# Moving the matmuls of a batch's value compression from the end of the batch before into three places of the batch's own first half

## The chip, the cores and the metric

The kernel runs on one core of one Trainium2 chip. The metric is the device time of one execution in microseconds, as the median of three runs. Everything is float32.

## The reference, cut to what matters

One inference step of a two-layer hybrid decoder, for a prompt of 512 tokens and a sample group of 8 batches with 8 new tokens each, on 2,048 past tokens. In every layer the sample group does, batch by batch, two kinds of attention:

```python
kvc = compress(gather(pool_cmp) + new, pe, w1, w2)     # 127 compressed keys and values from 16 pages
o_cmp, o_sel = nsa_global(q, pos, kvc, blocks)         # compressed scores choose 16 of 32 blocks, selected attention
o_win = window_sample(q_a, win_all)                    # last 512 rows
o_dil = dilated_sample(q_b, dil_all)                   # (128,1), (512,4), (2048,16)
y = merge(o_cmp, o_sel, o_win, gate, o_dil, w_out)

def compress(kv, pe, w1, w2):                          # separately for keys (s=0) and values (s=1)
    hid = silu(sum over 32 positions of (kv + pe) @ w1)
    return hid @ w2
```

The compressed keys are needed for the scores, and the scores for the choice of blocks. The compressed values are needed only for the last product of the compressed branch, `p_cmp @ kvc_values`.

## The kernel before, in words

Each layer has a projection, the prompt's attention (4 rounds of 12 steps), 8 batches of the sample group, and 36 units of output projection and MLP. The five engines run their own programs, written out by hand, and meet on counting semaphores. No scheduler decides an order: what stands first in an engine's program is done first, and a wait holds up all that is behind it on that engine.

For each batch TensorE (the PE rows) does, in this order: dilated scores of the first nine tiles (L1371), scores with the new keys (L1388), compressed keys (L1395) and values (L1401) from the hidden layer, compressed scores (L1408), window scores (L1409), new scores (L1412, L1413), the last four dilated tiles (L1371), the sum for the block choice (L1421), a transpose (L1425), selected scores in two halves (L1431), transposes of the window's probabilities (L1441) and the dilated ones (L1449), dilated outputs (L1463, with L1457 among them), compressed and window outputs (L1470 to L1473), transposes of the selected probabilities (L1480), selected outputs (L1496) and the placing of all outputs (L1508, L1513).

`compress(s, lo, hi, at)` (L1303) is the large product of the compression, `raw pages @ w1`. It is 16 steps of two matmuls for the keys (s = 0) and as many for the values (s = 1). The trace counts two PE records for each of these matmuls, so one compression is 64 records. Both compressions of batch b + 1 stand in the second half and at the end of batch b. Behind each, ScalarE takes an exponential (L744) and VectorE makes the hidden layer with an addition, a reciprocal and a product (L1935, L1937, L1939), which raises `h_done`. Those of the first batch of a layer stand among the last steps of the prompt's attention.

The raw pages of a batch lie in one buffer, `raw`, half of the tile `ring` (2 MB). There is no second one. SyncE (the SP queue) loads it. Its loop per batch is:

```python
page = page_numbers(b + 1)                              # 16 register loads
sp.wait_ge(h_full.sem, h_full.at(it, 2))                # both compressions of batch b have read raw
load_raw(page, range(0, 9))
sp.wait_ge(td_full.sem, td_full.at(it, TD_SD + 1))
load_dilated_k(b + 1)                                   # 1280 KB and 1024 KB
load_raw(page, range(9, NPG))
sp.wait_ge(win_pv.sem, ...); sp.wait_ge(od_full.sem, ...)
load_window(b + 1); load_dilated_v(b + 1, ...)
sp.wait_ge(oa_full.sem, ...); load_selected(page)
```

`h_full` is raised by the last matmul of each compression, once for the keys and once for the values of a batch. TensorE waits for all 16 pages (`raw_ld`) ahead of the first matmul of the next batch's key compression. The last four dilated key tiles are loaded by ScalarE's queue (L758), once the first five are used.

Of the kernel before, what the change touches and what calls it, by code (L numbers as in the profile page):

```python
# [22 lines left out]
ALU = mybir.AluOpType  # L23
ACT = mybir.ActivationFunctionType
# [3 lines left out]
P = 128  # L28
# [4 lines left out]
NB, NS = 8, 8  # L33
# [5 lines left out]
HD = 64  # L39
# [36 lines left out]
STEPS, ROUNDS = STEPS_A + STEPS_D, 4  # L76
# [5 lines left out]
TD_SD, TD_PTC, TD_PTW, TD_PTD, TD_PTS, TD_N = 0, 1, 2, 3, 4, 6  # L82
SC_KTC, SC_VC, SC_S, SC_WIN, SC_NEW, SC_IMP, SC_SEL, SC_LEAST, SC_SUM, SC_OUT, SC_N = (
    0, 1, 2, 3, 4, 5, 6, 8, 9, 10, 11)
SC_BANK = {SC_KTC: 2, SC_VC: 3, SC_S: 4, SC_WIN: 5, SC_NEW: 2, SC_IMP: 3, SC_SEL: 2, SC_SEL + 1: 3,
           SC_LEAST: 2, SC_SUM: 2, SC_OUT: 6}
HID_BANK, FIRST_HID = (4, 5), (2, 3)
EX_CMP, EX_WIN, EX_DIL, EX_SEL = 1, 2, 3, 4
# [96 lines left out]
def build(nc, i, o):  # L185
    ctx = ExitStack()
    with ctx:
# [23 lines left out]
        w2 = sb("w2", P, 2, HD)  # L211
# [350 lines left out]
        def _(act):  # L562
# [168 lines left out]
            with act.Fori(0, DEPTH) as l:  # L731
# [6 lines left out]

                def hidden_exp(it, at):

                    for s in range(2):
                        act.wait_ge(h_full.sem, h_full.at(it, s + 1))
                        act.wait_ge(h_done.sem, h_done.at(it, s))
                        nc.scalar.activation(  # L744
                            he.rearrange("p (k n) -> p k n", k=2),
                            bank[at[s]][:, 0:258].rearrange("p (k n) -> p k n", k=2)[:, :, 1:129],
                            ACT.Exp, scale=-1.0, bias=ncbias[:, s:s + 1]).then_inc(s_hexp.sem, 1)

                def batch(b):
# [14 lines left out]
                    act.wait_ge(td_used.sem, td_used.at(it, TD_SD + 1))  # L764
                    probs(s_d, 3, slice(0, P))
                    act.wait_ge(td_full.sem, td_full.at(it, TD_PTW + 1))
                    B = bank[TD_PTW % 2]
# [11 lines left out]

                hidden_exp(l * NB, FIRST_HID)  # L780
                with act.Fori(0, NB - 1) as b:
                    batch(b)
                    hidden_exp(l * NB + b + 1, HID_BANK)
                batch(NB - 1)
# [202 lines left out]
        def _(pe):  # L987
# [320 lines left out]
            def prompt_steps(l, g, first, last, ends):  # L1308

                for m in range(first, last):  # L1310
                    if m < STEPS or not ends:
                        step_scores(l, *in_round(g, m))
                    if m == 5:
                        chunk_scores(l, g)
                    if m >= TO_T and (m - TO_T < STEPS or not ends):
                        step_transposes(l, *in_round(g, m - TO_T))
                    if ends and m == STEPS:
                        pe.wait_ge(a_sb.sem, a_sb.at(l, 2 * STEPS_L))
                        pe.wait_ge(raw_ld.sem, raw_ld.at(l * NB, NPG))
                        pe.sem_inc(waits_taken_pe, 1)  # L1320
                        compress(0, 0, 4, FIRST_HID[0])
                    if ends and m == STEPS + 1:
                        compress(0, 8, 12, FIRST_HID[0])
                    if ends and m == STEPS + 2:
                        compress(1, 0, 4, FIRST_HID[1])
                    if m == 9:
                        chunk_probs_transposes(l, g)
                    if m >= TO_PV:
                        step_outputs(l, g, m - TO_PV)
                    if ends and m == STEPS:  # L1330
                        compress(0, 4, 8, FIRST_HID[0])
                    if ends and m == STEPS + 1:
                        compress(0, 12, 16, FIRST_HID[0])
                    if ends and m == STEPS + 2:
                        compress(1, 4, 8, FIRST_HID[1])
                    if m == 10:
                        chunk_outputs(l, g)
# [4 lines left out]
            with pe.Fori(0, DEPTH) as l:  # L1342
# [14 lines left out]
                def batch(it, more):  # L1357
# [39 lines left out]
                    last.then_inc(sc_full.sem, 1)  # L1397
                    pe.wait_ge(h_done.sem, h_done.at(it, 2))
                    B = bank[SC_BANK[SC_VC]]
                    for k in range(2):  # L1400
                        last = mm(B[:, k * HD:(k + 1) * HD], hid[:, 1, k * P:(k + 1) * P], w2[:, 1, :],  # L1401
                                  start=(k == 0), stop=(k == 1), skip_group_check=True)
                    last.then_inc(sc_full.sem, 1)

# [8 lines left out]
                    mm(B[low, 64:128], q_a, kns[:], start=True, stop=True, skip_group_check=True).then_inc(  # L1413
                        sc_full.sem, 1)

                    pe.wait_ge(kda_ld.sem, kda_ld.at(it, 2))
# [7 lines left out]
                    pe.sem_inc(waits_taken_pe, 1)  # L1424
                    tr(bank[TD_PTC % 2][:, 0:64], s_c, ident[0:64, 0:64]).then_inc(td_full.sem, 1)  # L1425

                    pe.wait_ge(sel_ld.sem, sel_ld.at(it, NPG))
                    for u in range(2):
                        pe.wait_ge(sc_used.sem, sc_used.at(it, (SC_NEW, SC_IMP)[u] + 1))
                        for h, rows in enumerate((low, high)):  # L1430
                            last = mm(bank[SC_BANK[SC_SEL + u]][rows, :], q_a,  # L1431
                                      kvsel[:, 8 * h + 4 * u:8 * h + 4 * u + 4, 0:128], start=True, stop=True,
                                      skip_group_check=True)
                        last.then_inc(sc_full.sem, 1)
                    pe.wait_ge(s_exp.sem, s_exp.at(it, EX_WIN))
                    pe.wait_ge(td_used.sem, td_used.at(it, 1))
# [36 lines left out]
                    mm(O[high], ptw[0:64, 4, :], vsm[:, 128:256], start=False, stop=True,  # L1473
                        skip_group_check=True).then_inc(win_pv.sem, 1)

# [10 lines left out]
                    if more:  # L1486
                        pe.wait_ge(raw_ld.sem, raw_ld.at(it + 1, NPG))
                        compress(0, 0, 3, HID_BANK[0])
                    O = bank[3][:, 0:P]
# [12 lines left out]
                    if more:  # L1502
                        compress(0, 3, 11, HID_BANK[0])
                    B = bank[SC_BANK[SC_OUT]]
# [44 lines left out]
        def _(dve):  # L1549
# [317 lines left out]
            with dve.Fori(0, DEPTH) as l:  # L1867
# [61 lines left out]

                def hidden_batch(it, at):  # L1930

                    horder = Order(ch_h, it)
                    for s in range(2):
                        dve.wait_ge(s_hexp.sem, s_hexp.at(it, s + 1))
                        V.tensor_scalar(he, he, 1.0, None, ALU.add).then_inc(horder.sem, 1)  # L1935
                        dve.wait_ge(horder.sem, horder.next())
                        V.reciprocal(he, he).then_inc(horder.sem, 1)  # L1937
                        dve.wait_ge(horder.sem, horder.next())
                        V.scalar_tensor_tensor(  # L1939
                            hid[:, s, :].rearrange("p (k n) -> p k n", k=2),  # L1940
                            bank[at[s]][:, 0:258].rearrange("p (k n) -> p k n", k=2)[:, :, 1:129], cbias[:, s:s + 1],
                            he.rearrange("p (k n) -> p k n", k=2), ALU.add, ALU.mult).then_inc(h_done.sem, 1)
                    if horder.k != 4:
                        raise ValueError(horder.k)

                def batch(b):
# [112 lines left out]

                hidden_batch(l * NB, FIRST_HID)  # L2060
                with dve.Fori(0, NB - 1) as b:
                    batch(b)
                    hidden_batch(l * NB + b + 1, HID_BANK)
                batch(NB - 1)
# [111 lines left out]
```

## Time and profile before

| | |
|---|---|
| median of three runs (lowest, highest) | 2443.39 us (2442.29, 2445.78) |
| the profiled execution's own time | 2435.86 us |
| its span in the profile | 2434.0 us |
| mean granted TensorE clock | 0.985 of full speed |
| PE matmul busy, share of the span | 94% |
| VectorE, GpSimd, ScalarE busy | 37%, 27%, 23% |
| DMA, mean over the span | 184 GB/s |
| the chain of work that ended last: PE, VectorE, issue, DMA, ScalarE | 84%, 5%, 5%, 3%, 2% |

The chain is the work followed back from the last instruction, at each step to what released it. Where an engine has a share of that chain, time taken from it can shorten the kernel. A busy share counts an engine's instructions and tells nothing of what they waited for.

### The profile page before, as it was taken

The page shows a single profiled execution, that of the slowest core. Times are in us where ns is not written, and L with a number is a line of the kernel's source. Part 1 is how long each engine was busy: PE and PEld are TensorE (multiplying, and loading weights), DVE is VectorE, ACT ScalarE, POOL GpSimd, SP SyncE. Part 2 cuts the span into 40 slices and gives each one's busy share as a digit, 9 for nine tenths or more (in the row PEclk, how much of TensorE's full clock was granted, in tenths as well). Part 3 has the DMA queues.
Part 4 walks back from the last instruction along what each step waited for, and adds up shares of the span by engine and source line. Part 5 has one row for each costly group of instructions (what it writes and reads, how often), then busy time and mean ns, then how long its engine had stood idle before and what let it go on. Part 6 is the DMA issues. An engine that isn't in the chain of part 4 may idle for free.

```text
span 2434.0 us, 43176 instructions
## 1 busy us (share of the span) xinstructions
PE 2291.6 (94%) x13534; PEld 1610.0 (66%) x13534; DVE 904.7 (37%) x2423; ACT 553.0 (23%) x1306; POOL 646.0 (27%) x719
## 2 busy tenths in 40 slices
PE   7999888898899999999999998889899999999998
PEld 4544556667666777777745455667667667777776
DVE  2002663434344232336510146443433532223374
ACT  2101651111112422120211036411111133222202
POOL 0000771000132343434100037510010524343441
PEclk9999999999999999999999999999999999999999
DMA  9542016777863454445365220277777644454441
GB/s 342 197 166 74 23 53 242 247 284 261 298 238 149 165 209 175 176 162 200 122 259 190 104 86 0 79 280 289 257 287 259 241 159 163 163 211 173 178 161 40
DMA packets 128529, 448.19 MB, mean 184 GB/s; under 512 B 17921, under 2 KB 89474, under 8 KB 107266
## 3 DMA queue, kind: packets, MB, share of 16 engines
q1 hardware_dynamic: 118768, 416.45, 47.0%
q10 hardware_dynamic: 9618, 29.98, 3.6%
q8 instruction: 71, 1.16, 0.2%
q14 instruction: 72, 0.59, 0.1%
HBM read 435.76 MB, written 152.57 MB: 242 GB/s over the span
## 4 chain that ended last, share of the span: by engine, by line
PE 84%; DVE 5%; issue 5%; DMA 3%; ACT 2%; DVEq 1%; ACTq 0%; SPq 0%; POOLq 0%
PE bank L1036 37%; PE bank L1119 16%; PE bank L1303 9%; PE bank L1463 3%; DMA zone<-in_dilated_k 2%; PE bank L1250 2%; PE bank L1238 2%; PE bank L1371 2%; PE bank L1270 2%; PE bank L1496 1%; ACT zone L682 1%; PE bank L1017 1%; PE bank L1135 1%; PE bank L1465 1%; PE bank L1480 1%
## 5 line engine op out<-in xcount | busy, mean ns | idle before, releaser
L1036 PE MATMUL bank<-zone,ring 128*128 128x288 f32 x1664 | 425.8, 408 | 7.8 <-DVE zone L1637 5.2
L1119 PE MATMUL bank<-ring,hT 128*128 128x512 f32 (+3 forms) x960 | 396.4, 566 | 6.5 <-ACTq L727 5.0
L1036 PEld LDWEIGHTS bank<-zone,ring 128*128 128x128 f32 x1664 | 315.6, 190 | 101.3 <-DVE zone L1637 10.7
L1036 PE MATMUL bank<-zone,w 128*128 128x288 f32 x1408 | 353.6, 406 | 0.0
L1036 PEld LDWEIGHTS bank<-zone,w 128*128 128x128 f32 x1408 | 267.5, 190 | 73.9
L1119 PEld LDWEIGHTS bank<-ring,hT 128*128 128x128 f32 (+1 forms) x960 | 168.9, 181 | 197.3 <-issue 183.1
L1303 PE MATMUL bank<-ring,w 128*128 128x128 f32 x2048 | 242.4, 277 | 0.0
L845 POOL TENSOR_TENSOR w<-ring 128x512 f32<-128x512 f32 x72 | 94.8, 1317 | 553.3 <-PE bank L1036 312.3
L1303 PEld LDWEIGHTS bank<-ring,w 128*128 128x128 f32 x2048 | 233.1, 192 | 3.8 <-issue 3.8
L956 POOL TENSOR_TENSOR zone<-constants,stat 128x1024 f32<-128x1024 f32 x16 | 30.4, 1897 | 522.8 <-DVE stat L2002 522.8
L607 ACT COPY zone<-bank 128x288 f32<-128x288 f32 x72 | 28.7, 398 | 563.4 <-PE bank L1036 563.4
L1036 PE MATMUL bank<-xT,ring 128*128 128x288 f32 x512 | 136.0, 409 | 2.0 <-ACT zone L607 2.0
L682 ACT ACTIVATE zone<-zone,stat 128x128 f32<-128x128 f32 (+1 forms) x192 | 106.2, 554 | 102.9 <-DVE stat L1779 102.9
L1036 PEld LDWEIGHTS bank<-xT,ring 128*128 128x128 f32 x512 | 97.2, 191 | 29.6 <-ACT zone L607 2.9
L848 POOL TENSOR_TENSOR w<-w,ring 128x512 f32<-128x512 f32 x72 | 109.5, 1522 | 13.4 <-POOL w L845 13.4
L1779 DVE CUSTOM_DVE_ANT_0 zone<-bank,zone 128x128 f32<-128x128 f32 (+1 forms) x192 | 86.4, 488 | 71.7 <-PE bank L1238 63.9
L874 POOL COPY zone<-zone 128x128 f32<-128x128 f32 (+1 forms) x24 | 9.7, 403 | 361.5 <-ACT zone L654 361.5
L599 ACT ACTIVATE ring<-ring,gains 128x256 f32<-128x256 f32 x256 | 105.3, 494 | 0.0
L852 POOL TENSOR_TENSOR w<-ring,w 128x512 f32<-128x512 f32 x72 | 99.8, 1386 | 12.8 <-POOL ring L849 11.1
L1250 PE MATMUL bank<-c_ident,zone 128*128 128x128 f32 x480 | 75.6, 282 | 25.9 <-ACT zone L692 23.6
L1250 PEld LDWEIGHTS bank<-c_ident,zone 128*128 128x128 f32 x480 | 51.8, 142 | 69.9 <-issue 67.6
L654 ACT ACTIVATE zone<-bank,stat 128x512 f32<-128x512 f32 (+3 forms) x50 | 32.4, 648 | 284.8 <-PE bank L1119 284.8
(250 smaller groups left out, 2818.1 us busy)
## 6 DMA issues: line engine op xcount, KB each, us to landing
out_dil_s<-in_state_kv_dil SPq DMA_DIRECT2D x48, 2720.0 KB, 12.2
ring<-in_w_units SPq DMA_DIRECT2D x72, 1024.0 KB, 4.8
zone<-in_dilated_v SPq DMA_DIRECT2D x16, 3072.0 KB, 10.6
ring<-in_cache_kv_cmp SPq DMA_DIRECT2D x256, 128.0 KB, 2.6
ring<-in_cache_kv_sel SPq DMA_DIRECT2D x256, 128.0 KB, 5.7
ring<-in_w_in SPq DMA_DIRECT2D x10, 2048.0 KB, 8.0
zone<-in_dilated_k SPq DMA_DIRECT2D x16, 1280.0 KB, 5.9
zone<-in_dilated_k SPq DMA_DIRECT2D x16, 1024.0 KB, 7.8
```

What stands on the lines that cost most here:

```text
L599: last = nc.scalar.activation(w_[:, h, k], w_[:, h, k], ACT.Copy, scale=gain_of(l * 2 + 1, 4 * h + k))
L682: nc.scalar.activation(p_sb[:, slot, k, 0:w], p_sb[:, slot, k, 0:w], ACT.Exp, scale=-1.0, bias=stat[:, 16 + at:17 + at], accum_out=stat[:, ...
L845: nc.gpsimd.tensor_tensor(c_[:, 0], w_[:, 2], w_[:, 3], ALU.add).then_inc(s_comb.sem, 1)
L848: nc.gpsimd.tensor_tensor(c_[:, 1], c_[:, 0], w_[:, 0], ALU.subtract).then_inc(s_comb.sem, 1)
L852: nc.gpsimd.tensor_tensor(c_[:, 2], w_[:, 1], c_[:, 1], ALU.subtract).then_inc(s_comb.sem, 1)
L1036: last = mm(dst[:, 0:HALF], lhs[:, k, :], rhs(k), start=first and k == 0, stop=(k == 3), skip_group_check=True)
L1119: last = mm(dst, hT[:, k, t * P:t * P + ROWS[t]], ring[:, n % 2, k * CH:k * CH + width], start=start and k == 0, stop=stop and k == KT - 1)
L1238: last = mm(bank[2 * (m % 2) + k][:, 0:w], q[rows, t * P:(t + 1) * P], kT[rows, 0:w], start=True, stop=True)
L1250: last = tr(bank[4 + k][:, c * P:(c + 1) * P], p_sb[:, slot, k, c * P:(c + 1) * P], ident[:])
L1303: last = mm(out[:, k, first:first + P], w1[:, s, j, :], rawt[:, :, s, k, j % 8, :], start=(j == 0 and k == 0), stop=(j == 15 and k == 1), ...
L1463: mm(bank[7][32 * g:32 * g + M, :], ptd[:, e, at:at + M], vd[:, j, :], start=(j == 0), stop=False, skip_group_check=True)
L1779: V.tensor_tensor_reduce(p_sb[:, slot, k, 0:w], bank[2 * (m % 2) + k][:, 0:w], (p_bias if m < STEPS_A else p_biasd)[:, k, SEQ - w:SEQ], -1 ...
```

## The change

Only TensorE's, ScalarE's and VectorE's programs change. SyncE's and GpSimd's stay as they are, with the same waits on the same semaphores.

- The value compression of a batch no longer stands at the end of the batch before (and for the first batch of a layer no longer in the prompt's last steps and ahead of the loop). It is cut into three pieces in the batch's own first half: steps 0 to 5 behind the new scores, 6 to 10 behind the choice's sum and transpose, 11 to 15 behind the selected scores. It goes to bank 6.
- The hidden layer of the values (ScalarE's exponential, VectorE's three operations) moves with it: ScalarE's behind the exponential of the dilated scores, VectorE's behind the maximum of the selected scores.
- The small product of the values (`w2`) and its copy move from the batch's start to behind the dilated outputs. The compressed output follows the window's.

```diff
-HID_BANK, FIRST_HID = (4, 5), (2, 3)
+HID_BANK, FIRST_HID, VHID_BANK = 4, 2, 6
+V_AHEAD, V_NEW, V_CHOICE, V_SEL = 0, 6, 11, 16
...
                     probs(s_d, 3, slice(0, P))
+                    hidden_exp(it, 1, VHID_BANK)
                     act.wait_ge(td_full.sem, td_full.at(it, TD_PTW + 1))
...
-                    if ends and m == STEPS + 2:
-                        compress(1, 0, 4, FIRST_HID[1])
...
-                    if ends and m == STEPS + 2:
-                        compress(1, 4, 8, FIRST_HID[1])
...
                     last.then_inc(sc_full.sem, 1)
-                    pe.wait_ge(h_done.sem, h_done.at(it, 2))
-                    B = bank[SC_BANK[SC_VC]]
-                    for k in range(2):
-                        last = mm(B[:, k * HD:(k + 1) * HD], hid[:, 1, k * P:(k + 1) * P], w2[:, 1, :],
-                                  start=(k == 0), stop=(k == 1), skip_group_check=True)
-                    last.then_inc(sc_full.sem, 1)
...
+                    pe.wait_ge(sc_used.sem, sc_used.at(it, 0))
+                    pe.wait_ge(og_a.sem, og_a.at(l, ROUNDS))
+                    pe.sem_inc(waits_taken_pe, 1)
+                    compress(1, V_AHEAD, V_NEW, VHID_BANK)
...
                     tr(bank[TD_PTC % 2][:, 0:64], s_c, ident[0:64, 0:64]).then_inc(td_full.sem, 1)
+                    compress(1, V_NEW, V_CHOICE, VHID_BANK)
...
                         last.then_inc(sc_full.sem, 1)
+                    compress(1, V_CHOICE, V_SEL, VHID_BANK)
                     pe.wait_ge(s_exp.sem, s_exp.at(it, EX_WIN))
...
-                    pe.wait_ge(sc_used.sem, sc_used.at(it, 0))
+                    pe.wait_ge(sc_used.sem, sc_used.at(it, SC_LEAST + 1))
+                    pe.wait_ge(h_done.sem, h_done.at(it, 2))
+                    B = bank[SC_BANK[SC_VC]]
+                    for k in range(2):
+                        last = mm(B[:, k * HD:(k + 1) * HD], hid[:, 1, k * P:(k + 1) * P], w2[:, 1, :],
+                                  start=(k == 0), stop=(k == 1), skip_group_check=True)
+                    last.then_inc(sc_full.sem, 1)
                     O = bank[6][:, 0:P]
-                    mm(O[low], ptc, vc, start=True, stop=True, skip_group_check=True)
...
+                    pe.wait_ge(sc_used.sem, sc_used.at(it, SC_VC + 1))
+                    pe.sem_inc(waits_taken_pe, 1)
+                    mm(O[low], ptc, vc, start=True, stop=True, skip_group_check=True).then_inc(win_pv.sem, 1)
...
                     if more:
-                        compress(0, 11, 16, HID_BANK[0])
-                        compress(1, 0, 16, HID_BANK[1])
-
-                compress(1, 8, 16, FIRST_HID[1])
+                        compress(0, 11, 16, HID_BANK)
+
...
-                    V.tensor_copy(vc, small(SC_VC)[:, 0:P]).then_inc(sc_used.sem, 1)
...
                     dve.sem_inc(s_max.sem, 1)
+                    hidden_batch(it, 1, VHID_BANK)
...
+                    V.tensor_copy(vc, small(SC_VC)[:, 0:P]).then_inc(sc_used.sem, 1)
                     dve.wait_ge(od_full.sem, od_full.at(it, 1))
```

TensorE, first half of a batch, from the new scores to the second half of the selected scores. In the rows, `ring,w` is a compression, `ring,q_s` a selected score, `zone 32x128` a dilated one. Before:

```order
L1413 MATMUL bank<-kns,q_s 64x64
L1416 REGISTER_ALU
L1371 MATMUL bank<-zone 32x128 [waits dilated_ka_loaded]
L1371 MATMUL bank<-zone 32x128 x15
L1421 MATMUL bank<-zone,gs 128x128 [waits group_sums_scaled]
L1425 MATMUL bank<-c_ident,zone 128x64 [waits bank01_used]
L1427 ISA
L1429 REGISTER_ALU [waits selected_loaded]
L1431 MATMUL bank<-ring,q_s 64x512 [waits small_banks_used]
L1431 MATMUL bank<-ring,q_s 64x512
```

And after the change:

```order
L1405 MATMUL bank<-kns,q_s 64x64
L1407 REGISTER_ALU
L1305 MATMUL bank<-ring,w 128x128 [waits small_banks_used,sparse_pair_kept]
L1305 MATMUL bank<-ring,w 128x128 x11
L1412 REGISTER_ALU
L1369 MATMUL bank<-zone 32x128 [waits dilated_ka_loaded]
L1369 MATMUL bank<-zone 32x128 x15
L1417 MATMUL bank<-zone,gs 128x128 [waits group_sums_scaled]
L1421 MATMUL bank<-c_ident,zone 128x64 [waits bank01_used]
L1305 MATMUL bank<-ring,w 128x128 x10
```

Twelve matmuls now stand ahead of the last dilated tiles and ten behind the transpose; a third piece of ten stands behind the selected scores, and its last matmul is the one that raises `h_full` for the second time.

TensorE, end of a batch, from the selected outputs' last product to the loop's branch. Before:

```order
L1500 MATMUL bank<-vsm,zone 64x128 [waits small_banks_used]
L1303 MATMUL bank<-ring,w 128x128 x16
L1508 MATMUL bank<-constants,zone 128x8 [waits sparse_out_scaled,dilated_out_scaled]
L1508 MATMUL bank<-constants,zone 128x8 x3
L1513 MATMUL bank<-constants,zone 128x32
L1513 MATMUL bank<-constants,zone 128x32 [waits sparse_out_scaled]
L1303 MATMUL bank<-ring,w 128x128 x42
```

And after the change:

```order
L1505 MATMUL bank<-vsm,zone 64x128 [waits small_banks_used]
L1305 MATMUL bank<-ring,w 128x128 x16
L1513 MATMUL bank<-constants,zone 128x8 [waits sparse_out_scaled,dilated_out_scaled]
L1513 MATMUL bank<-constants,zone 128x8 x3
L1518 MATMUL bank<-constants,zone 128x32
L1518 MATMUL bank<-constants,zone 128x32 [waits sparse_out_scaled]
L1305 MATMUL bank<-ring,w 128x128 x10
```

The 42 matmuls at the end (10 of the keys, 32 of the values) become the 10 of the keys.

SP's queue in a batch, the same before and after (the rows of before; nine and seven pages are single rows there):

```order
L527 ISA
L478 ISA [waits hidden_full]
L478 DMA ring<-in_cache_kv_cmp 128x256
L478 ISA
L478 DMA ring<-in_cache_kv_cmp 128x256
...
L496 ISA [waits bank01_full]
L496 DMA zone<-in_dilated_k 128x2560
L497 ISA
L497 DMA zone<-in_dilated_k 128x2048
L478 ISA
L478 DMA ring<-in_cache_kv_cmp 128x256
```

Nothing moved here, but `hidden_full` now reaches its second count within the batch and not ahead of it.

## Rows read from the trace of the kernel before

**Rows 1.** The page: the chain that ended last, share of the span by engine.
```profile
PE 84%; DVE 5%; issue 5%; DMA 3%; ACT 2%; DVEq 1%; ACTq 0%; SPq 0%; POOLq 0%
```
**Rows 2.** Waits of PE, whole span: waiting line, releaser, us in total, times, longest.
```profile
PE bank L1371 <- DMA zone<-in_dilated_k: 24.9, 20, 2.8
PE bank L1431 <- DVE topk L1994: 17.3, 16, 1.5
PE bank L1449 <- DVE zone L2006: 14.5, 16, 1.0
```
**Rows 3.** Timeline of PE, one batch: start, us, line, xrecords, [idle before <-releaser].
```profile
515.56 2.94 PE L1371 MATMUL bank<-zone 128*128 128x128 f32 x72
...
519.83 0.66 PE L1401 MATMUL bank<-w,zone 128*128 128x64 f32 x4
...
522.82 1.08 PE L1371 MATMUL bank<-zone 128*32 128x128 f32 x32 [1.20 <-DMA zone<-in_dilated_k]
...
526.44 1.08 PE L1431 MATMUL bank<-ring,q_s 128*64 128x512 f32 x4 [1.07 <-DVE topk L1994]
...
528.92 0.66 PE L1449 MATMUL bank<-c_ident,zone 128*128 128x128 f32 x4 [0.96 <-DVE zone L2006]
530.39 2.08 PE L1463 MATMUL bank<-zone 128*128 128x512 f32 x10 [0.81 <-ACT zone L773]
...
538.53 1.58 PE L1303 MATMUL bank<-ring,w 128*128 128x128 f32 x12
...
547.24 9.62 PE L1303 MATMUL bank<-ring,w 128*128 128x128 f32 x84
556.70 0.50 PE L1371 MATMUL bank<-zone 128*128 128x128 f32 x3
```
**Rows 4.** Stretches: us, PE, PEld, DVE, ACT, POOL busy, clock, DMA share, GB/s.
```profile
471.77:515.56 43.79, 39.74 (x378) 29.02 (x376) 16.11 (x53) 6.05 (x15) 3.12 (x9) 0.92 0.73 263
515.56:556.70 41.14, 37.06 (x377) 28.55 (x376) 16.11 (x53) 6.05 (x15) 3.12 (x9) 1.00 0.78 280
...
384.46:680.12 295.66, 267.43 (x2625) 201.74 (x2626) 111.51 (x370) 41.89 (x104) 21.84 (x63) 0.97 0.77 278
1582.34:1877.98 295.64, 266.71 (x2626) 201.22 (x2626) 111.62 (x370) 41.89 (x104) 21.85 (x63) 0.97 0.77 278
680.12:709.32 29.20, 25.31 (x250) 14.65 (x248) 14.14 (x49) 5.58 (x14) 11.93 (x9) 0.88 0.58 208
1877.98:1904.53 26.55, 22.63 (x250) 14.18 (x248) 14.77 (x49) 5.58 (x14) 10.16 (x8) 1.00 0.62 227
```
**Rows 5.** Timeline of DVE: first and last operation of a batch's value hidden layer.
```profile
516.27 0.29 DVE L1935 TENSOR_SCALAR zone<-zone 128x256 f32<-128x256 f32 x1 [4.47 <-ACT zone L744]
...
518.38 0.48 DVE L1939 SCALAR_TENSOR_TENSOR zone<-bank,cbias,zone 128x256 f32<-128x256 f32 x1
```
**Rows 6.** Timeline of SP's queue, around and in the same batch.
```profile
501.39 7.83 SPq L478 DMA_DIRECT2D ring<-in_cache_kv_sel  x16
...
520.47 5.18 SPq L478 DMA_DIRECT2D ring<-in_cache_kv_cmp  x9
525.99 0.33 SPq L496 DMA_DIRECT2D zone<-in_dilated_k  x1
...
530.77 0.33 SPq L478 DMA_DIRECT2D ring<-in_cache_kv_cmp  x1
```
**Rows 7.** DMA issues from 530.7 to 530.9: KB each, us from issue to landing.
```profile
ring<-in_cache_kv_cmp SPq DMA_DIRECT2D x1, 128.0 KB, 6.4
```
**Rows 8.** Two us of the same batch, columns as in rows 4 (last: GB/s).
```profile
531.56:533.56 2.00, 1.96 (x18) 0.53 (x14) 1.14 (x7) 0.27 (x1) 0.19 (x2) 1.00 0.95 396
```
**Rows 9.** Timelines of PE and SP at the first batch of layer 1.
```profile
374.78 2.05 PE L1303 MATMUL bank<-ring,w 128*128 128x128 f32 x16
...
384.46 0.71 PE L1371 MATMUL bank<-zone 128*128 128x128 f32 x4 [2.84 <-DMA zone<-in_dilated_k]
...
378.73 0.33 SPq L496 DMA_DIRECT2D zone<-in_dilated_k  x1
```

More of the change, by code:

```diff
@@ L82 @@
 TD_SD, TD_PTC, TD_PTW, TD_PTD, TD_PTS, TD_N = 0, 1, 2, 3, 4, 6
-SC_KTC, SC_VC, SC_S, SC_WIN, SC_NEW, SC_IMP, SC_SEL, SC_LEAST, SC_SUM, SC_OUT, SC_N = (
-    0, 1, 2, 3, 4, 5, 6, 8, 9, 10, 11)
+SC_KTC, SC_S, SC_WIN, SC_NEW, SC_IMP, SC_SEL, SC_LEAST, SC_VC, SC_SUM, SC_OUT, SC_N = (
+    0, 1, 2, 3, 4, 5, 7, 8, 9, 10, 11)
 SC_BANK = {SC_KTC: 2, SC_VC: 3, SC_S: 4, SC_WIN: 5, SC_NEW: 2, SC_IMP: 3, SC_SEL: 2, SC_SEL + 1: 3,
            SC_LEAST: 2, SC_SUM: 2, SC_OUT: 6}
-HID_BANK, FIRST_HID = (4, 5), (2, 3)
+HID_BANK, FIRST_HID, VHID_BANK = 4, 2, 6
+V_AHEAD, V_NEW, V_CHOICE, V_SEL = 0, 6, 11, 16
 EX_CMP, EX_WIN, EX_DIL, EX_SEL = 1, 2, 3, 4
@@ L737, in _, with hidden_exp @@
                 prompt_steps(l, ROUNDS - 1, AHEAD, STEPS + AHEAD, True)
[L739 to L747, printed above, removed]
+                def hidden_exp(it, s, at):
+                    act.wait_ge(h_full.sem, h_full.at(it, s + 1))
+                    act.wait_ge(h_done.sem, h_done.at(it, s))
+                    act.sem_inc(waits_taken_act, 1)
+                    nc.scalar.activation(
+                        he.rearrange("p (k n) -> p k n", k=2),
+                        bank[at][:, 0:258].rearrange("p (k n) -> p k n", k=2)[:, :, 1:129],
+                        ACT.Exp, scale=-1.0, bias=ncbias[:, s:s + 1]).then_inc(s_hexp.sem, 1)
                 def batch(b):
@@ L778, in batch @@
                     copy(pts[:, 4:8, :].rearrange("p c r -> p (c r)"), bank[(TD_PTS + 1) % 2][:]).then_inc(pts_act.sem, 1)
-                hidden_exp(l * NB, FIRST_HID)
+                hidden_exp(l * NB, 0, FIRST_HID)
                 with act.Fori(0, NB - 1) as b:
                     batch(b)
-                    hidden_exp(l * NB + b + 1, HID_BANK)
+                    hidden_exp(l * NB + b + 1, 0, HID_BANK)
                 batch(NB - 1)
@@ L1320, in prompt_steps @@
                         pe.sem_inc(waits_taken_pe, 1)
-                        compress(0, 0, 4, FIRST_HID[0])
+                        compress(0, 0, 4, FIRST_HID)
                     if ends and m == STEPS + 1:
-                        compress(0, 8, 12, FIRST_HID[0])
-                    if ends and m == STEPS + 2:
-                        compress(1, 0, 4, FIRST_HID[1])
+                        compress(0, 8, 12, FIRST_HID)
                     if m == 9:
@@ L1330, in prompt_steps @@
                     if ends and m == STEPS:
-                        compress(0, 4, 8, FIRST_HID[0])
+                        compress(0, 4, 8, FIRST_HID)
                     if ends and m == STEPS + 1:
-                        compress(0, 12, 16, FIRST_HID[0])
-                    if ends and m == STEPS + 2:
-                        compress(1, 4, 8, FIRST_HID[1])
+                        compress(0, 12, 16, FIRST_HID)
                     if m == 10:
@@ L1466, in batch @@
                        skip_group_check=True).then_inc(od_full.sem, 1)
-                    pe.wait_ge(sc_used.sem, sc_used.at(it, 0))
+                    pe.wait_ge(sc_used.sem, sc_used.at(it, SC_LEAST + 1))
[5 more added lines that the diff above has]
+                    last.then_inc(sc_full.sem, 1)
                     O = bank[6][:, 0:P]
-                    mm(O[low], ptc, vc, start=True, stop=True, skip_group_check=True)
                     for c in range(4):
                         mm(O[high], ptw[:, c, :], kw_sb[:, c, 128:256], start=(c == 0), stop=False, skip_group_check=True)
-                    mm(O[high], ptw[0:64, 4, :], vsm[:, 128:256], start=False, stop=True,
-                        skip_group_check=True).then_inc(win_pv.sem, 1)
+                    mm(O[high], ptw[0:64, 4, :], vsm[:, 128:256], start=False, stop=True, skip_group_check=True)
+                    pe.wait_ge(sc_used.sem, sc_used.at(it, SC_VC + 1))
+                    pe.sem_inc(waits_taken_pe, 1)
+                    mm(O[low], ptc, vc, start=True, stop=True, skip_group_check=True).then_inc(win_pv.sem, 1)
                     pe.wait_ge(s_exp.sem, s_exp.at(it, EX_SEL))
@@ L1487, in batch @@
                         pe.wait_ge(raw_ld.sem, raw_ld.at(it + 1, NPG))
-                        compress(0, 0, 3, HID_BANK[0])
+                        compress(0, 0, 3, HID_BANK)
                     O = bank[3][:, 0:P]
@@ L1502, in batch @@
                     if more:
-                        compress(0, 3, 11, HID_BANK[0])
+                        compress(0, 3, 11, HID_BANK)
                     B = bank[SC_BANK[SC_OUT]]
@@ L1928, in _, with hidden_batch @@
                 prompt_steps(l, ROUNDS - 1, AHEAD, STEPS + AHEAD, True)
[L1930 to L1943, printed above, removed]
+                def hidden_batch(it, s, at):
+                    horder = Order(ch_h, it, 2 * s)
+                    dve.wait_ge(s_hexp.sem, s_hexp.at(it, s + 1))
+                    dve.sem_inc(waits_taken_dve, 1)
+                    V.tensor_scalar(he, he, 1.0, None, ALU.add).then_inc(horder.sem, 1)
+                    dve.wait_ge(horder.sem, horder.next())
+                    V.reciprocal(he, he).then_inc(horder.sem, 1)
+                    dve.wait_ge(horder.sem, horder.next())
+                    V.scalar_tensor_tensor(
+                        hid[:, s, :].rearrange("p (k n) -> p k n", k=2),
+                        bank[at][:, 0:258].rearrange("p (k n) -> p k n", k=2)[:, :, 1:129], cbias[:, s:s + 1],
+                        he.rearrange("p (k n) -> p k n", k=2), ALU.add, ALU.mult).then_inc(h_done.sem, 1)
+                    if horder.k != 2:
                         raise ValueError(horder.k)
@@ L2058, in batch @@
                         raise ValueError((order.k, lay.k))
-                hidden_batch(l * NB, FIRST_HID)
+                hidden_batch(l * NB, 0, FIRST_HID)
                 with dve.Fori(0, NB - 1) as b:
                     batch(b)
-                    hidden_batch(l * NB + b + 1, HID_BANK)
+                    hidden_batch(l * NB + b + 1, 0, HID_BANK)
                 batch(NB - 1)
```

## Prediction, written before the changed kernel was run

> **What bounds the kernel now.** I read the chain first: PE holds 84% of it [rows 1], so only what stands in PE's order, or makes PE wait, counts. The list of PE's waits comes next, since the change fills PE's waits in the batches [rows 2]: 24.9 us for dilated keys, 17.3 us in the middle of the selected scores, 14.5 us ahead of the dilated transposes. Then the timeline of one batch shows where each lies [rows 3]: the batch that starts at 515.56 and hands over at 556.70 waits 1.20, 1.07, 0.96 and 0.81 us, all in its first 15 us. From here times "at +x" count from a batch's start, so the last dilated tiles are at +7.26, the dilated outputs at +14.83, the next batch's key compression (behind the wait for the raw pages) at +22.97, the end at +41.14. No wait stands at +22.97. The table of stretches shows batches of two kinds [rows 4]: 41.14 us at full granted clock, and 43.79 us with a mean clock of 0.92. By the PE timeline, 7 of the 16 batches have such a low stretch, each dearer by about 2.65 us. It follows the first half, where the waits are.
>
> **The change, part by part.** A record of the compression costs 9.62 / 84 = 0.1145 us [rows 3].
> - Taken from a batch's end: 64 records, 7.33 us.
> - The small value product (four records, 519.83 to 520.42) leaves its place: 0.59 us. It covered VectorE's copy of the keys, for which PE waits next, so a wait of the same length takes its place: 0 gained.
> - First piece, 24 records, 2.75 us, ahead of a wait of 1.20: +1.55. The tiles are loaded by ScalarE's queue at the old moment, so that wait is gone.
> - Second piece, 20 records, 2.29 us, ahead of a wait of 1.07: +1.22. VectorE's choice is released by the dilated tiles and so is late with them, but ends 3.6 us after their start as now (522.82 to 526.4), and PE gets to the second selected score 4.8 us after it.
> - Third piece, 20 records, 2.29 us, ahead of a wait of 0.96: +1.33. ScalarE's new exponential is released as this piece ends and is done before or with the window transposes; I charge 0.15 for it. The 0.81 us ahead of the dilated outputs stay, as those are ScalarE's copies of the transposes just made.
> - So the dilated outputs start at +14.83 + 4.25 = +19.08.
> - VectorE's value hidden layer takes 2.6 us [rows 5], started by the small product L1457 some 2 us into the outputs. It ends with the outputs, within 0.2 us. The small value product behind it costs 0.59 again. Together +0.75.
> - The point where PE needs the raw pages moves to 22.97 + 4.25 + 0.75 = +27.97. With nothing in the way a batch would take 41.14 + 5.0 - 7.33 = 38.8 us, 2.3 us less than a full-clock batch, and the low stretches would go too.
>
> **What is in the way.** The pages' loads wait for the second count of `h_full`, because the one raw buffer is read until then. Before, it came at the end of the batch before, and was no limit: SP's queue issued selected pages until 509.2, then spent 11.2 us on the page numbers, and issued the first raw page at 520.47, +4.91 [rows 6]. Now the third piece ends at +11.9 + 2.77 + 2.29 = +17.0 (+11.9 is the old end of the selected scores), and the first page can go at about +17.3, as the page numbers are done by then. From first issue to the landing of the last page is 530.77 + 6.4 - 520.47 = 16.7 us [rows 6, 7]: nine pages, two dilated tiles of 1280 and 1024 KB, then seven pages behind these. So the last page lands at +34.0, against a need at +27.97: **a new wait of 6.0 us in every batch that has a successor**, at the head of the key compression. Before, the pages landed 1.4 us ahead of need (537.2 against 538.53).
>
> Bounds of those 16.7 us: 4.46 MB at the 396 GB/s of [rows 8] would be 11.3 us, but nine pages go out at the pace of their issue (520.47 to 525.99, 5.5 us) and the 3.28 MB behind take 8.3: 13.8 us at least, a wait of 3.1. Above, I take 17.4. I take 16.7, as queue, order and sizes are the same. The window and value loads are issued behind the pages; the selected pages go out later but land by +4 of the next batch, needed at +12.6.
>
> The clock: the low batches cost 2.65 us with their waits spread. A 6 us wait with nothing in it should bring a stretch at 1.2 GHz (the lower of the two levels) each time, part of which falls in the wait; a stretch of about 7 us (0.08 x 43.79 / 0.5) wholly on work would cost 3.5. I take 1.6, ends 0 and 3.5. For 0 speaks that the 2.84 us wait at a layer's start [rows 9] is followed by no drop. The Trainium skill (TensorE: Matmul & The Clock Gate, HAM oscillation — how this bites in real kernels) says that waits for DMA between bursts make each next burst start at the low clock. By that rule the loss comes in all 14 batches; by the row of the layer's start it would be nil.
>
> **The sum.** A batch with a successor: 34.0 + 0.1, then the rest behind the wait, 41.14 - 22.97 - 7.33 = 10.84, and 1.6 for the clock: 46.5 us. Seven of these per layer: 325.5, against 295.66 and 295.64 [rows 4]. At a layer's start the removed pieces (two of 16 records, about 2 us each [rows 9]) let the dilated keys be asked for about 3.65 us sooner (before at 378.73), and the batch starts that much sooner, though behind a longer idle stretch; with its second wait I charge 1.4. Per layer 325.5 + 1.4 - 3.65 - 295.65 = +27.6. The last batch of a layer has no page wait, but now holds its value compression: +5.0, less the 2.65 that layer 1 lost to the clock [rows 4]: together +7.35. Its unit weights come later (they wait for the same count) but before use. Total 2 x 27.6 + 7.35 = **+62.6 us**. The profiled execution, 2435.9, is 7.5 us under the median; on the median 2443.4 this gives 2506.
>
> **Rivals.**
> - *The clock stays up.* Same wait, but no loss behind it: 44.9 us a batch, 2 x (314.3 + 0.4 - 3.65 - 295.65) + 7.35 = +38 us, 2482. Chance 0.22.
> - *The pages come in time, and it is faster.* If the pages landed within 28.0 - 17.3 = 10.7 us of the first issue, the filled waits would be kept: 38.8 us a batch, 2 x (271.6 + 0.4 - 3.65 - 295.65) + 7.35 = -47 us, 2396. For it: three waits really end in the filled places, and the low stretches go with them. Against it: 10.7 us is below even the bandwidth's 11.3. Chance 0.10.
> - *The transfer speeds up to its 13.8 us and the clock stays up.* 42.0 us a batch: 2 x (294 + 0.4 - 3.65 - 295.65) + 7.35 = -2 us. Chance 0.08.
> - The change does what it says otherwise: the order of instructions shows the pieces where the diff puts them.
>
> **How the numbers follow.** Forecast 0.60 (2506), the others 0.22, 0.10, 0.08. A measurement of this kernel tells about 0.2%, 5 us. Slower: 0.60 + 0.22 + 0.02 of the last case; same 0.04; faster 0.10 + 0.02. The range takes in the forecast with the clock's upper end (48.4 us a batch, +90, 2534) and the second case with a transfer 1.2 us shorter (43.7 a batch, +21, 2464). It leaves out the two cases without a loss.
>
> **What would show it.** Right: a PE wait of about 6 us on a DMA of `in_cache_kv_cmp` ahead of the key compression, 14 times; the waits of [rows 2] for dilated keys in mid-batch, for L1994 and L2006 gone; first raw page issued at about +17; batches of 44.5 to 47 us; the lower granted clock now behind the page wait and no longer in the dilated outputs. Wrong: no such wait and batches near 39 us. If batches are near 45 and the clock stays 1.00 behind the wait, only the clock's term was off.

## The result, and the profile after

The changed kernel took 2513.77 us (median of 4 runs, 2510.78 to 2516.97) against 2442.84 for the kernel before: **2.9% slower**, ratio 1.0293 with a 95% interval of 1.0271 to 1.0314. A second set gave 1.0304 (1.0271 to 1.0338). The forecast was +62.6 us, measured is +70.9. One execution of run 5 below was in a slower state of the chip (2688.58 us at a granted clock of 0.846) and is left out of its ratio.

The page, engines' busy times and the chain that ended last:

```profile
span 2512.7 us, 43272 instructions
...
PE 2329.7 (93%) x13534; PEld 1654.8 (66%) x13534; DVE 905.0 (36%) x2423; ACT 551.4 (22%) x1306; POOL 647.7 (26%) x719
...
PE 81%; issue 5%; SPq 5%; DMA 4%; DVE 3%; ACT 2%; DVEq 0%; ACTq 0%; POOLq 0%
```

PE has as many records as before. But the chain, which had 0% of SP's queue in [rows 1], now runs 5% through it: SP has come onto the path though its program was not touched. PE's waits (who waited <- releaser: us in total, times, longest) say where:

```profile
PE bank L1305 <- DMA ring<-in_cache_kv_cmp: 70.6, 14, 5.3
...
PE bank L1369 <- DMA zone<-in_dilated_k: 12.7, 2, 6.4
...
PE bank L1470 <- DVE zone L1942: 8.4, 16, 0.5
PE bank L1400 <- DVE zone L1974: 8.1, 16, 0.5
```

The three groups of [rows 2] are gone from the middle of the batches (the dilated keys keep one wait per layer, at its first batch). In their place stand 14 waits for raw pages, 5.0 us each. The timeline of PE for one batch, which starts at 528.38 and answers to [rows 3]:

```profile
528.38 2.94 PE L1369 MATMUL bank<-zone 128*128 128x128 f32 x72
...
533.23 0.32 PE L1400 MATMUL bank<-zone,q_s 128*64 128x128 f32 x1 [0.50 <-DVE zone L1974]
...
534.35 2.94 PE L1305 MATMUL bank<-ring,w 128*128 128x128 f32 x24
537.23 1.08 PE L1369 MATMUL bank<-zone 128*32 128x128 f32 x32
...
538.71 2.50 PE L1305 MATMUL bank<-ring,w 128*128 128x128 f32 x20
541.14 1.94 PE L1428 MATMUL bank<-ring,q_s 128*64 128x512 f32 x8
543.01 2.50 PE L1305 MATMUL bank<-ring,w 128*128 128x128 f32 x20
...
547.27 2.11 PE L1461 MATMUL bank<-zone 128*128 128x512 f32 x10 [0.72 <-ACT zone L775]
...
553.10 0.63 PE L1470 MATMUL bank<-w,zone 128*128 128x64 f32 x4 [0.52 <-DVE zone L1942]
...
562.01 2.93 PE L1305 MATMUL bank<-ring,w 128*128 128x128 f32 x12 [5.03 <-DMA ring<-in_cache_kv_cmp]
...
575.31 2.94 PE L1369 MATMUL bank<-zone 128*128 128x128 f32 x72
```

The first half did what the change was to do: the dilated tiles at 537.23 and the eight records of selected scores run through without a stop. The price stands at 562.01. SP's queue in the same batch, to be read beside [rows 6], and the landing of the last page (issues in 555.8 to 556.3: KB, us to landing):

```profile
545.79 4.87 SPq L479 DMA_DIRECT2D ring<-in_cache_kv_cmp  x9
551.00 0.33 SPq L497 DMA_DIRECT2D zone<-in_dilated_k  x1
...
555.84 0.33 SPq L479 DMA_DIRECT2D ring<-in_cache_kv_cmp  x1
...
ring<-in_cache_kv_cmp SPq DMA_DIRECT2D x1, 128.0 KB, 6.1
```

The first page is issued at 545.79, +17.41 from the batch's start, 0.3 us behind the end of the third piece, and the last lands at 561.9, +33.6. Stretches (columns as in [rows 4]): that batch, its wait, the first 6.8 us behind it, the first batch and the seven batches of each layer, then the two last batches:

```profile
528.38:575.31 46.93, 40.15 (x377) 31.30 (x376) 16.01 (x53) 5.94 (x15) 3.12 (x9) 0.93 0.69 249
...
556.97:562.01 5.04, 0.01 (x2) 0.01 (x1) 0.45 (x3) 0.14 (x1) 0.00 (x0) 0.80 1.05 390
562.01:568.85 6.84, 6.84 (x53) 6.27 (x54) 0.35 (x1) 0.00 (x0) 0.00 (x0) 0.65 1.05 449
716.15:748.36 32.21, 30.46 (x314) 21.85 (x312) 15.74 (x52) 5.94 (x15) 6.94 (x5) 1.00 0.59 209
1950.57:1982.74 32.17, 30.43 (x313) 21.83 (x312) 15.72 (x52) 5.94 (x15) 6.92 (x5) 1.00 0.59 206
385.11:716.15 331.04, 283.85 (x2625) 221.46 (x2626) 109.56 (x368) 41.10 (x104) 21.86 (x63) 0.92 0.69 247
1619.23:1950.57 331.34, 283.42 (x2626) 220.91 (x2627) 109.58 (x368) 41.09 (x104) 21.84 (x63) 0.92 0.68 247
```

In the wait PE is empty and the DMA engines are full (share 1.05, 390 GB/s); behind it the granted clock averages 0.65, so most of that stretch runs at 1.2 GHz. Seven batches take 331.0 and 331.3 us against 295.7 and 295.6 [rows 4].

### The profile page after: what moved, and what is told of

Read it like the earlier page. It is cut to its first block, busy times and chain, and to the rows that moved or that the text cites. A ratio compares the mean times of both kernels' runs of the same rounds, so it can differ in the third digit from the quotient of the medians.

```text
span 2512.7 us, 43272 instructions
## 1 busy us (share of the span) xinstructions
PE 2329.7 (93%) x13534; PEld 1654.8 (66%) x13534; DVE 905.0 (36%) x2423; ACT 551.4 (22%) x1306; POOL 647.7 (26%) x719
## 4 chain that ended last, share of the span: by engine, by line
PE 81%; issue 5%; SPq 5%; DMA 4%; DVE 3%; ACT 2%; DVEq 0%; ACTq 0%; POOLq 0%
PE bank L1038 36%; PE bank L1121 15%; PE bank L1305 11%; SPq L479 4%; DMA ring<-in_cache_kv_cmp 3%; PE bank L1369 3%; PE bank L1252 2%; PE bank L1240 2%; PE bank L1501 2%; PE bank L1272 2%; PE bank L1428 1%; ACT zone L683 1%; PE bank L1019 1%; PE bank L1137 1%; PE bank L1386 1%
## 5 line engine op out<-in xcount | busy, mean ns | idle before, releaser
L1305 PE MATMUL bank<-ring,w 128*128 128x128 f32 x2048 | 272.5, 292 | 70.6 <-DMA ring<-in_cache_kv_cmp 70.6
L1305 PEld LDWEIGHTS bank<-ring,w 128*128 128x128 f32 x2048 | 253.2, 203 | 90.7 <-DMA ring<-in_cache_kv_cmp 71.8
L851 POOL TENSOR_TENSOR ring<-ring 128x512 f32<-128x512 f32 x72 | 96.1, 1335 | 0.0
```

What stands on the lines that cost most here:

```text
L851: nc.gpsimd.tensor_tensor(w_[:, 2], w_[:, 0], w_[:, 2], ALU.subtract).then_inc(s_comb.sem, 1)
L1305: last = mm(out[:, k, first:first + P], w1[:, s, j, :], rawt[:, :, s, k, j % 8, :], start=(j == 0 and k == 0), stop=(j == 15 and k == 1), ...
```

## The experiments

Each ratio is against runs of the kernel before on the same chip (2440 to 2443 us). Differences from the changed kernel are taken from its 2513.77 us above, which was timed apart from runs 1 to 8; the kernel before took 2442.84 there.

**1. The pages ahead of the dilated keys** (the changed kernel otherwise):

```diff
-                    load_raw(page, range(0, 9))
+                    load_raw(page, range(NPG))
                     sp.wait_ge(td_full.sem, td_full.at(it, TD_SD + 1))
                     load_dilated_k(b + 1)
-                    load_raw(page, range(9, NPG))
```

> The changed kernel, but SP issues all 16 raw pages first and the two dilated key tiles behind them. If the page wait is the loss: the last page lands about 17.4 + 16 x 0.54 + 2.3 = +28.4 us into the batch, where PE needs it at +28.6, so the wait of 5.0 us before the key compression shrinks to under 0.5 us, the low clock behind it goes, and a batch takes 39.4 to 40 us instead of 46.9. Total about 14 x 7 = 100 us less: 2405 to 2420 us. If the loss lies in the order of PE's work itself (the pieces in the first half, the clock), the time stays near 2514.

Measured: 2433.91 us, ratio 0.9974 (0.9953 to 0.9994), 80 us less than the changed kernel. Of the 14 waits for pages one of 0.9 us is left, and no granted clock below full is left inside the loop after a layer's first batch. But most batches take 40.9 to 41.3 us (40.5 to 42.3 in all), not the 39.4 to 40 expected, and the kernel misses its 2405 to 2420: a wait appeared that I had not foreseen, for the last four dilated tiles, which ScalarE's queue loads (PE's timeline, then SP's queue):

```profile
516.16 1.08 PE L1368 MATMUL bank<-zone 128*32 128x128 f32 x32 [1.55 <-DMA zone<-in_dilated_k]
```

```profile
539.76 13.32 SPq L479 DMA_DIRECT2D ring<-in_cache_kv_sel  x16
```

Issuing the 16 selected pages takes 13.3 us here, against 7.8 in [rows 6]: all that SP loads for a batch is now asked for in the second half of the one before. From the batch's start to these tiles (505.69 to 516.16) the DMA engines are full (share 1.03, 387 GB/s). So the theory held for the page wait, and the DMA engines' backlog was the next limit; run 5 tests that.

**2. No page loads inside the loop:**

```diff
-                    load_raw(page, range(0, 9))
...
-                    load_raw(page, range(9, NPG))
...
-                        pe.wait_ge(raw_ld.sem, raw_ld.at(it + 1, NPG))
```

> The changed kernel without the loads of the compression's pages for the batches after a layer's first (those batches compress the first batch's pages again). It leaves out work of the DMA queues, not of any engine. If the page wait is the whole loss, batches take 39.4 us at full clock and the kernel 2405 to 2415 us, and pages_first cannot beat it by much. If the wait only hid another one that ends as late, batches stay above 42 us.

Measured: 2406.54 us, ratio 0.9865 (0.9846 to 0.9884). Batches behind the second of a layer take 39.5 us. This is what the new order of PE's work gives when its data are there: better than the kernel before by 34 us. The kernel leaves out 2 MB of loads per batch, which by itself could have helped the other loads, but run 5, with every load in place, comes out the same. The order itself is no loss.

**3. PE kept busy in the wait:**

```diff
                     if more:
+                        for _ in range(21):
+                            mm(bank[5][:, 0:P], w1[:, 0, 0, :], w1[:, 0, 1, :], start=True, stop=True,
+                               skip_group_check=True)
                         pe.wait_ge(raw_ld.sem, raw_ld.at(it + 1, NPG))
```

> The changed kernel with 21 extra matmuls (4.8 us at full clock) that nobody reads, ahead of the wait for the pages. The pages land at the same moment, so the wait is filled but not shortened. If the clock's loss comes from PE standing still in that wait, batches fall from 46.9 to about 44.5 us and the kernel by 14 x 2.4 = 34 us to about 2480. If the slow work behind the wait has another cause, it stays at 2514 or rises.

Measured: 2484.72 us, ratio 1.0191 (1.0173 to 1.0208), 29 us under the changed kernel. Batches of 44.4 to 44.9 us after each layer's first. The timeline of PE, extra matmuls (`w`) and the key compression behind them:

```profile
547.90 4.93 PE L1493 MATMUL bank<-w 128*128 128x128 f32 x42
553.14 1.60 PE L1305 MATMUL bank<-ring,w 128*128 128x128 f32 x12 [0.30 <-DMA ring<-in_cache_kv_cmp]
```

Twelve records take 1.60 us here and 2.93 behind an empty wait: matmuls whose result nobody reads made the kernel 29 us faster. Filling the wait takes 2.3 us from a batch (46.9 to 44.6). So of the roughly 7.4 us by which a changed batch (46.9) exceeds one without the page wait (39.5), about 2.3 are the clock's and 5.0 the wait's.

**4. The whole value compression in one piece**, behind the new scores:

```diff
-V_AHEAD, V_NEW, V_CHOICE, V_SEL = 0, 6, 11, 16
+V_AHEAD, V_NEW, V_CHOICE, V_SEL = 0, 16, 16, 16
...
-                if hi == 16:
+                if hi == 16 and lo < hi:
```

The second line keeps an empty piece from raising `h_full`.

> The changed kernel with all 16 steps of the value compression in the first place, behind the new scores. The raw buffer is then free at about +13.5 instead of +17.1, and the pages land at about +30.0, while PE needs them at +30.5, as the two waits of about 1 us in the selected scores and the dilated transposes come back. If the release of the raw buffer governs the wait, it goes: batches of 41.3 us (43.9 where the clock is low), 2435 to 2460 us. If the filled waits were what mattered, this would be slower than the changed kernel, above 2514.

Measured: 2450.10 us, ratio 1.0039 (1.0019 to 1.0058), 64 us under the changed kernel. Its waits of PE:

```profile
PE bank L1447 <- DVE zone L2008: 15.2, 16, 1.0
PE bank L1428 <- DVE topk L1996: 14.7, 16, 1.1
```

The two waits of about 1 us are back, the 5 us one is gone: the release of the raw buffer, 3.7 us sooner (first page at +13.68 instead of +17.41), is worth more than both filled waits. All batches but each layer's first take 41.3 to 43.4 us, the dearer ones with a low stretch of the clock; 41.3 and 43.9 were worked out.

**5. The dilated keys ahead of the wait for the raw buffer:**

```diff
+                    sp.wait_ge(td_full.sem, td_full.at(it, TD_SD + 1))
+                    load_dilated_k(b + 1)
                     sp.wait_ge(h_full.sem, h_full.at(it, 2))
...
+                    load_raw(page, range(NPG))
```

> The changed kernel, but SP issues the two dilated key tiles ahead of the wait for the raw buffer (at about +12, when the DMA engines have nothing to do) and then all 16 pages. pages_first left a wait of 1.4 to 1.6 us for the last dilated tiles in each batch, at 41.1 us a batch. If that wait comes from 6 MB (keys, window, values, selected pages) queued behind the pages, it goes here: no PE wait on a DMA inside the loop over 0.3 us, batches of 39.5 us as in pages_once, 2405 to 2418 us. If it has another cause, such as the order of ScalarE's queue, batches stay at 41.1 us and the kernel at about 2434.

Measured: 2406.91 us, ratio 0.9856 (0.9829 to 0.9884); **it beats both kernels**. Stretches of two batches, and SP's queue:

```profile
505.35:545.10 39.75, 37.88 (x378) 29.13 (x376) 16.02 (x53) 5.94 (x15) 3.12 (x9) 1.00 0.80 290
545.10:584.70 39.60, 37.84 (x377) 29.09 (x376) 16.00 (x53) 5.94 (x15) 3.12 (x9) 1.00 0.80 289
```

```profile
517.41 0.34 SPq L497 DMA_DIRECT2D zone<-in_dilated_k  x1
...
522.76 8.82 SPq L479 DMA_DIRECT2D ring<-in_cache_kv_cmp  x16
...
538.08 7.84 SPq L479 DMA_DIRECT2D ring<-in_cache_kv_sel  x16
```

The keys go at +12, into an idle stretch of the DMA engines (their share from 513.00 to 517.40 is 0.00), and the selected pages are issued in 7.8 us again. The wait for the last dilated tiles is gone with it. Once more beside the next run and the changed kernel:

> keys_before_pages once more, beside keys_first_cover_copy on the same chip: 2403 to 2412 us, 14 to 17 parts in a thousand under the kernel before.

> The changed kernel once more beside these two, so that all three are compared on one chip: 2510 to 2517 us, 2.8 to 3.1% over the kernel before.

Measured: 2410.71 us, 0.9877 (0.9852 to 0.9902), and 2516.22 us, 1.0304.

**6. PE kept busy at a layer's start**, on the kernel of 5:

```diff
+                for _ in range(28):
+                    mm(bank[1][:, 0:P], w1[:, 0, 0, :], w1[:, 0, 1, :], start=True, stop=True, skip_group_check=True)
                 with pe.Fori(0, NB - 1) as b:
```

> keys_before_pages with 28 extra matmuls (6.4 us) that nobody reads ahead of each layer's first batch, where PE stands still for 6.4 us because the value compression no longer covers the load of the dilated keys. The load is as late as before, so only the clock can change: if the slow first dilated scores (5.0 to 5.6 us for 72 records in the changed kernel, against 2.9 in other batches) come from PE standing still, the first batches fall by about 2.5 us each and the kernel by about 5. If not, no change or some tenths more.

Measured: 2419.12 us, ratio 0.9912 (0.9879 to 0.9945): no gain, rather slower. The timeline of PE without (layer 2) and with the extra matmuls (layer 1):

```profile
1566.22 5.65 PE L1368 MATMUL bank<-zone 128*128 128x128 f32 x72 [6.37 <-DMA zone<-in_dilated_k]
```

```profile
381.64 6.52 PE L1524 MATMUL bank<-w 128*128 128x128 f32 x56
388.25 2.17 PE L1368 MATMUL bank<-zone 128*128 128x128 f32 x40
392.09 1.08 PE L1368 MATMUL bank<-zone 128*32 128x128 f32 x32 [1.67 <-DMA zone<-in_dilated_k]
```

The scores do run at 2.4 GHz now (40 records in 2.17 us), but then wait 1.7 us for the second load of dilated keys, whose landing the slow scores had covered. That accounts for most of the missing gain. Of the 12 us between the two profiled spans (2418.2 and 2406.2), 3.6 are a low stretch that fell later in layer 2's first batch (45.9 us against 42.2), and 3.7 lie ahead of layer 1's extra matmuls (they start at 381.64; without them PE's wait starts at 377.95). In both first batches PE also waits for pages again, 0.9 and 1.3 us. The rest, and what brings the low stretch, stay open. My guess of 2.5 us a layer was wrong.

**7. The kernel before, with its three short waits filled:**

```diff
+                    for _ in range(5):
+                        mm(bank[6][:, 0:P], ident[:], ident[:], start=True, stop=True, skip_group_check=True)
                     pe.wait_ge(kda_ld.sem, kda_ld.at(it, 2))
```

and likewise four ahead of each of the two others.

> The kernel before, with 5, 4 and 4 extra matmuls that nobody reads in its three waits of about 1 us in a batch's first half. Nothing is moved and no wait is shortened. If the 43.8 us batches of the kernel before are the 41.1 us ones at a lower clock that PE's short waits bring about, all batches take 41.1 to 41.4 us, and the kernel gets 7 x 2.65 = 18 us faster, about 2423. If they have another cause, it stays at 2441.

Measured: 2430.63 us, ratio 0.9954 (0.9936 to 0.9973), 12 runs. Two batches:

```profile
473.46:514.70 41.24, 40.26 (x404) 31.68 (x403) 16.10 (x53) 6.05 (x15) 3.12 (x9) 1.00 0.78 280
514.70:555.80 41.10, 40.25 (x403) 31.64 (x402) 16.11 (x53) 6.05 (x15) 3.12 (x9) 1.00 0.78 281
```

All batches after each layer's first take 41.1 to 41.4 us; none of 43.8 is left there. So the two kinds of batch of the kernel before are one kind at two clocks, and waits of about 1 us each were enough for the lower one. Of the 18 us worked out, 9 show in the kernel's time. In the profiles the 16 batches together take 12.4 us less (634.6 against 647.0). One low stretch is left: it begins in the wait at layer 1's start and slows the first scores behind it, which took 3.6 us at this place in the kernel before:

```profile
387.79 5.64 PE L1371 MATMUL bank<-zone 128*128 128x128 f32 x72 [2.74 <-DMA zone<-in_dilated_k]
```

That batch takes 44.4 us. The rest is lost outside the batches, where nothing was changed and where the same kernel's profiles differ by some us from run to run (layer 1's first batch starts at 384.40 in run 5 and at 380.19 in its repeat).

**8. Two steps of the value compression ahead of the compressed scores**, on the kernel of 5:

```diff
+                    compress(1, V_AHEAD, 2, VHID_BANK)
...
-                    compress(1, V_AHEAD, V_NEW, VHID_BANK)
+                    compress(1, 2, V_NEW, VHID_BANK)
```

> keys_before_pages with the first two of the value compression's 16 steps (0.92 us) moved from behind the new scores to ahead of the compressed scores, where PE waits 0.5 us for VectorE's copy of the keys since the small value product left that place. If that wait is real and nothing else ends as late, it goes from all 16 batches: 39.2 us a batch instead of 39.7, 8 us in all. If VectorE's chain behind the scores, now 0.4 us later, decides, no change.

Measured: 2410.43 us, ratio 0.9865 (0.9834 to 0.9896). Behind a layer's second batch it did what was expected: 39.1 to 39.4 us against 39.5 to 39.8, and no wait between the two rows below. Over all 16 batches the profile gives 4.1 us less than for the kernel of 5 beside it (621.4 against 625.5), half of the 8 worked out. In the kernel's time its six runs spread over 2400 to 2418 and the comparison cannot tell it from the kernel of 5.

```profile
507.11 1.16 PE L1304 MATMUL bank<-ring,w 128*128 128x128 f32 x8
508.20 0.32 PE L1404 MATMUL bank<-zone,q_s 128*64 128x128 f32 x1
```

## Why the prediction was right, and which terms were mis-sized

The mechanism, its place and its count were as forecast; runs 1, 2, 4 and 5 show it from four sides, since each takes away the page wait in another way and regains 64 to 107 us. Step by step:

- **First page and last page.** Forecast +17.3 and +34.0, measured +17.41 and +33.6. The transfer took 16.2 us instead of 16.7.
- **Where PE needs it.** Forecast +27.97, measured 556.97 - 528.38 = +28.59. Two terms were too small. The wait for the values' hidden layer, put at up to 0.2, is 0.52 in all 16 batches: VectorE starts it only 0.5 us after the start of the one-column operation it stands behind (549.84 and 550.35). And the move of the compressed output behind the window's, put at nothing, costs 0.37. Before, the two outputs ran side by side in 1.0 us (535.71 to 536.73); after, the window's take the same 1.0 (553.66 to 554.67) and the compressed ones their own 0.37 behind (555.03 to 555.40). Against these stands that the dilated outputs start 0.2 sooner than forecast. Before, then after:

```profile
535.71 0.32 PE L1470 MATMUL bank<-zone 128*64 128x128 f32 x1
535.72 0.32 PE L1472 MATMUL bank<-zone 128*64 128x128 f32 x1
```

```profile
553.66 1.09 PE L1475 MATMUL bank<-zone 128*64 128x128 f32 x8
554.67 0.43 PE L1476 MATMUL bank<-vsm,zone 64*64 64x128 f32 x2
555.03 0.43 PE L1479 MATMUL bank<-zone 128*64 128x128 f32 x2
```

- **The page wait.** 6.0 forecast, 5.0 measured: 0.4 less at one end, 0.6 more at the other.
- **The clock behind it.** 1.6 forecast, measured 575.31 - 562.01 - 10.84 = 2.5. Of that 0.2 is not the clock's: at full clock, in run 3, the same work takes 11.04 (553.14 to 564.18), which leaves 2.3. This was the term with the widest bounds (0 to 3.5). The rival in which the clock stays up fell: in all 14 batches with a page wait a low stretch began in that wait and ran on into the work, and run 3 took it away. That is also what the Trainium skill states (TensorE: Matmul & The Clock Gate, HAM oscillation — how this bites in real kernels): a wait for DMA ahead of each burst starts each burst at the low clock. The trace agrees, with 12 records in 2.93 us instead of 1.58. The row that spoke for 0, the wait at a layer's start, was weaker than it looked: in run 7 the same wait, 2.74 us, did bring the low clock.
- **A batch.** 46.5 forecast, 46.9 and 47.1 measured (means of the six behind each layer's first, 45.9 to 47.8 singly): 0.4 less to the landing and 0.9 more behind it cancel in part, which is luck. The late need itself costs nothing here, as the pages are later still.
- **A layer's start.** 3.65 us sooner forecast. From the last transposes of the prompt to the first batch it took 13.24 us before (371.22 to 384.46) and 9.34 now (375.77 to 385.11): 3.9 sooner; 3.9 in layer 2 too. But the first batch costs 49.6 and 48.9, which is 2.7 and 1.9 more than the others instead of 1.4: its first scores run at the lower clock (72 records in 5.02 and 5.65 us, not 2.94).
- **The last batch.** 31.55 forecast, 32.2 measured: the 0.52 us wait and the 0.37 us again. The unit weights were no limit, as forecast.

The sum by layer: -3.9 + 35.4 + 3.0 = 34.5 and -3.9 + 35.7 + 5.6 = 37.4, together 71.9 us. The spans of the two profiles, from which these terms are read, differ by 78.7. 4.55 us of that lie ahead of anything that was moved (the prompt's last transposes at 375.77 instead of 371.22), the other 2.2 between layer 1's batches and layer 2's start and behind the last batch. The medians differ by 70.9, so that 71.9 comes this near them is in part luck. The forecast fell 8 to 9 us short by both, most of it in the batches.

The faster rival, whose condition was pages within 10.7 us of the first issue, did not come about in the changed kernel. Its gain was set too high: -47 forecast, -34 in run 2, where the pages are no condition at all; 39.5 us a batch instead of 38.8 makes 10 of the 13 us. The zero for the small value product's old place was right: the wait at L1400 (0.50) is about as long as the product it replaced (0.59), and run 8 shows that it can be filled.

## What to carry to other kernels

Before work is moved later, list what its last instruction releases, not only what it waits for: here the moved matmuls were the last readers of the only buffer for the next batch's input, and 12.5 us of prefetch time went with them (first page at +17.41 instead of +4.91). Compare the transfer's whole time, from first issue to last landing (16 us), with what is left between release and need (11 us). If the move is worth it in itself (it is, by 34 us), change the order of the loads with it: what does not need the buffer goes ahead of the wait for it. Whether the kernel before would gain from that order of loads alone was not run.

## What the runs showed that was not expected

- Short waits suffice to lower TensorE's clock. In the kernel before, waits of 1.2, 1.1, 1.0 and 0.8 us, with work between them (in a layer's first batch up to 1.55), were followed by low stretches in 7 of 16 batches, and filling three of them ended that (run 7). In run 4, with waits of 0.85, 0.95 and 0.72 us, they came in 8 of 16. The Trainium skill (TensorE: Matmul & The Clock Gate, Why this matters for your kernels) warns of long gaps between bursts of matmuls; here it was several short ones near each other.
- A single wait does not decide it by its length alone. Those at a layer's start, with dense work on both sides, took 2.84 and 2.73 us in the kernel before [rows 9] and 2.74 and 2.69 us in run 7. Only the 2.74 us one was followed by slow scores. What tells them apart these runs do not show.
- Matmuls whose result nobody reads paid: 21 in each batch made the changed kernel 29 us faster.
- A slow engine can cover a transfer: at a layer's start, running the first scores at the higher clock only brought out the wait for the next tiles (run 6).
